# Reordering the head and the layer boundary of a two-layer decoder trunk, with constant products on TensorE in its gaps

## The reference

```python
mod = silu(c) @ w_ada + b_ada                       # 1024 x 3072 per layer
shift, scale, gate = split(mod, 3)
h = rms_norm(x, norm_g) * (1.0 + scale) + shift
proj = h @ w_in                                     # q | k | v | za | u | zs
ya = attend(rope(q), rope(k), v, sinks)             # window 128, with sinks
ys = s5_branch(u, state, a_re, a_im, log_dt, b, c, d, w_glu, b_glu)   # complex diagonal SSM + GLU
x = x + gate * (concat(ya * silu(za), ys * silu(zs)) @ w_out)
```

## Time and profile before

| | us |
|---|---|
| median of 3 runs | 403.86 |
| lowest, highest | 399.94, 405.77 |
| the profiled execution | 400.8 |
| its span, first to last instruction | 399.0 |
| TensorE busy in it | 359.9 |
| VectorE busy | 316.1 |
| ScalarE busy | 197.2 |
| GpSimd busy | 64.8 |

### The profile page before, as it was taken

One profiled execution on the slowest core, in us unless ns is written; L12 is line 12 of the kernel. 1 busy time (PEld: TensorE's weight loads), 2 busy tenths in 40 slices (PEclk: granted clock), 3 DMA queues, 4 the chain that ended last, 5 costly groups with the idle time before them and its releaser, 6 DMA issues. The chain is left out here.

```text
span 399.0 us, 8243 instructions
## 1 busy us (share of the span) xinstructions
PE 359.9 (90%) x3122; PEld 313.2 (79%) x3122; DVE 316.1 (79%) x676; ACT 197.2 (49%) x423; POOL 64.8 (16%) x58
## 2 busy tenths in 40 slices
PE   0997589998999799999999759999999999899993
PEld 0462379987979597977989758999997988779992
DVE  1648889977899958898599876889699589976863
ACT  2365255365463117787335556427633177863432
POOL 3200000020000370000499800000000000002430
PEclk9999969999999899999999959999999999999998
DMA  8999826799839966953995072391998279522303
GB/s 247 292 349 369 203 60 229 244 169 204 264 101 267 268 176 168 352 125 92 294 301 103 2 235 67 91 167 46 287 176 214 45 202 334 142 64 59 100 2 131
DMA packets 125125, 72.27 MB, mean 181 GB/s; under 512 B 63385, under 2 KB 111605, under 8 KB 124990
## 3 DMA queue, kind: packets, MB, share of 16 engines
q1 hardware_dynamic: 111118, 65.05, 61.3%
q10 hardware_dynamic: 13968, 6.69, 7.3%
HBM read 64.74 MB, written 6.59 MB: 179 GB/s over the span
## 5 line engine op out<-in xcount | busy, mean ns | idle before, releaser
L691 PE MATMUL bank<-h_hi,w_hi 128*128 128x320 f32 x448 | 138.6, 322 | 13.0 <-DVE h_lo L1906 10.7
L691 PE MATMUL bank<-h_lo,w_hi 128*128 128x320 f32 x448 | 134.4, 312 | 0.0
L691 PEld LDWEIGHTS bank<-h_hi,w_hi 128*128 128x128 f32 x448 | 85.6, 191 | 21.0 <-issue 12.4
L691 PEld LDWEIGHTS bank<-h_lo,w_hi 128*128 128x128 f32 x448 | 85.7, 191 | 0.2
L691 PE MATMUL bank<-h_hi,w_lo 128*128 128x320 f32 x448 | 81.8, 312 | 0.0
L1702 DVE TENSOR_TENSOR w_lo<-raw,w_hi 128x1024 fp32r<-128x1024 f32 x50 | 63.0, 1259 | 10.7 <-ACT w_hi L1272 10.4
L691 PEld LDWEIGHTS bank<-h_hi,w_lo 128*128 128x128 f32 x448 | 70.9, 191 | 0.0
L1272 ACT ACTIVATE w_hi<-raw 128x1024 fp32r<-128x1024 f32 x50 | 52.7, 1053 | 31.0 <-DMA raw<-in_w_in 16.9
L2304 POOL TENSOR_TENSOR ga<-xT,fing 128x320 f32<-128x320 f32 x4 | 6.5, 1632 | 141.8 <-DVE xT L2185 141.8
L1452 ACT ACTIVATE R<-R,sm 128x128 f32<-128x128 f32 (+2 forms) x40 | 17.7, 443 | 9.6 <-issue 5.7
L691 PE MATMUL bank<-R,Gm 128*128 128x96 f32 x128 | 17.4, 297 | 3.8 <-DVE R L2039 3.8
(11 more groups left out here) (321 smaller groups left out, 638.1 us busy)
## 6 DMA issues: line engine op xcount, KB each, us to landing
R<-in_w_ada SPq DMA_DIRECT2D x34, 512.0 KB, 6.6
raw<-in_w_in SPq DMA_DIRECT2D x32, 256.0 KB, 5.9
raw<-in_w_in SPq DMA_DIRECT2D x14, 512.0 KB, 6.2
raw<-in_w_out SPq DMA_DIRECT2D x32, 128.0 KB, 3.6
raw<-in_w_out SPq DMA_DIRECT2D x16, 256.0 KB, 4.0
raw<-in_w_ada SPq DMA_DIRECT2D x4, 512.0 KB, 8.2
R<-in_w_in SPq DMA_DIRECT2D x4, 512.0 KB, 11.4
raw<-in_w_glu SPq DMA_DIRECT2D x4, 512.0 KB, 4.4
```

The source lines that it names most:

```text
L691: return nc.tensor.matmul(out_, lhsT, rhs, start=start, stop=stop, skip_group_check=free)
```

## The change

- **SyncE's queue:** ss0 and ss1 go behind the ten small loads; ss0 to ss7 stand together; the two loads of B (256 KB each) go from before ss6 to behind ss11.
- **TensorE, constant products:** `stay_busy(bank, n, cols)` multiplies the constant `mean` (128 x 128) by constants into a bank whose next job overwrites it. 12 of 128 columns stand ahead of c's turning, 5 of 128 ahead of x's, 3 of 512 ahead of `carried(0)` in layer 0, and at the boundary 1 of 512 ahead of `sum_squares`, 1 ahead of `spread_root` and 2 behind it.
- **TensorE, order:** `spread_root` after five chunks; `turn_modulation(0, 0)` right behind it; u0 and u1's tiles 0, 1 after ss7, tiles 2, 3 after ss9; B is turned after u0 and u1 are done, in the `work` ring. WB blocks of layer 0 are turned two each behind u3, q0, q1, q2.
- **ScalarE:** both am0 and am1 are copied out before w_hi of u0 and u1; the exponential of `ssm_sines` and the sines stand between am2 and am3; `inputs_B` comes behind u0's copy.
- **VectorE:** one more pair of squares is added ahead of `first_squares`, which has two products per group for three. Angles, `normed` of tiles 4 to 7 and `powers` stand between tiles 3 and 4; only four small operations (`denominators`) stand ahead of `normed`. `higher_powers` goes behind all tiles of h, followed by w_lo of u2, `inputs_scaled`, the four `turned_inputs`, and `wide_powers` last. In layer 1 `normed` is done two tiles at a time.
- **Sums of squares in both layers:** the last square is no longer added by VectorE; TensorE adds it with a third product per group.

```diff
+TURNED_AFTER = ({"u3": (0, 1), "q0": (2, 3), "q1": (4, 5), "q2": (6, 7)},
...
             sp.dma_start(crow[1:CT, :], a["c_sample"]).then_inc(cond_in, 16)
-            for m in range(2):
-                load(0, f"ss{m}")
...
-            for m in range(2, 6):
+            for m in range(8):
+                load(0, f"ss{m}")
+            sp.wait_ge(*work.ready(0, "cT"))
+            load(0, "u0")
+            load(0, "u1")
+            for m in range(8, 12):
                 load(0, f"ss{m}")
             for r, name in enumerate(("ssm_b_re", "ssm_b_im")):
...
-            for m in range(6, 8):
-                load(0, f"ss{m}")
-            sp.wait_ge(*work.ready(0, "cT"))
-            load(0, "u0")
-            load(0, "u1")
-            for m in range(8, 16):
+            for m in range(12, 16):
                 load(0, f"ss{m}")
...
+            def stay_busy(bank, n, cols=512):
+
+                for _ in range(n):
+                    mm(bank[:, 0:cols], mean[:, :], (const if cols > P else mean)[:, 0:cols], True, True)
+
+            pe.wait_ge(mean_set, 1)
+            b = work.bank(0, "cT")
+            stay_busy(b, 12, P)
...
             ins.then_inc(work.filled(0, "cT"), 1)
+            stay_busy(work.bank(0, "xT0"), 5, P)
             pe.wait_ge(x_in, 32)
...
                     mm(o, sqsum[:, toks], mean[:, 0:1], True, False)
+                    mm(o, sq[:, 0, toks], mean[:, 0:1], False, False)
                     ins = mm(o, sq[:, 1, toks], mean[:, 0:1], False, True)
...
                     first_squares()
-                    turn_inputs_B()
-                    for m in range(2, 4):
+                    for m in range(2, 5):
                         modulation(0, f"ss{m}")
                     spread_root(0)
-                    for m in range(4, 8):
+                    turn_modulation(0, 0)
+                    for m in range(5, 8):
                         modulation(0, f"ss{m}")
-                        if m == 5:
-                            turn_modulation(0, 0)
                     turn_modulation(0, 1)
-                    for m in range(8, 12):
-                        modulation(0, f"ss{m}")
                     project_two(0, ("u0", "u1"), range(2), True)
-                    turn_modulation(0, 2)
-                    for m in range(12, 14):
+                    for m in range(8, 10):
                         modulation(0, f"ss{m}")
                     project_two(0, ("u0", "u1"), range(2, 4), True)
-                    for m in range(14, 16):
+                    for m in range(10, 12):
+                        modulation(0, f"ss{m}")
+                    turn_modulation(0, 2)
+                    for m in range(12, 16):
                         modulation(0, f"ss{m}")
                     turn_modulation(0, 3)
                     project_two(0, ("u0", "u1"), range(4, KT), False)
+                    turn_inputs_B()
                     turn_inputs_C()
...
+                    pe.wait_ge(*work.room(l, "rms"))
+                    stay_busy(work.bank(l, "rms"), 1)
                     sum_squares(l, "rms", l + 1)
...
+                    pe.wait_ge(*proj.room(l, "u0"))
+                    stay_busy(proj.bank(l, "u0"), 1)
                     spread_root(l)
+                    stay_busy(proj.bank(l, "u0"), 2)
                     project_two(l, ("u0", "u1"), range(KT), True)
...
+                pe.wait_ge(*work.room(l, "y0"))
+                if l == 0:
+                    stay_busy(work.bank(l, "y0"), 3)
                 pe.wait_ge(H_ready, (l + 1) * 2)
...
             def ssm_sines():
 
                 act.wait_ge(ssm_exp, 3)
+                fn(zz[:, 6, :], zz[:, 4, :], ACT.Exp).then_inc(ssm_val, 1)
...
                 if l == 0:
-                    inputs_B()
                     modulation_rows(0, 0)
-                    ssm_sines()
+                    modulation_rows(0, 1)
                     hi_part(0, 0)
-                    modulation_rows(0, 1)
                     hi_part(0, 1)
                 for pair in range(0, KT, 2):
-                    if l == 0 and pair in (2, 4):
-                        modulation_rows(0, 2 if pair == 2 else 3)
+                    if l == 0 and pair == 4:
+                        modulation_rows(0, 2)
+                        ssm_sines()
+                        modulation_rows(0, 3)
...
                 newton(l + 1)
                 if l == 0:
-                    powers()
+                    denominators()
                 dve.wait_ge(*work.ready(l, "rb"))
...
-                    if pair == 4:
+                    if l:
+                        normed((pair, pair + 1))
+                    elif pair == 4:
+                        angles()
                         normed(range(4, KT))
                         if l == 0:
-                            higher_powers()
+                            powers()
                             modulation_of(0, 2)
                             modulation_of(0, 3)
...
                 if l == 0:
+                    higher_powers()
+                    lo_part(0, 2)
                     inputs_scaled()
+                    for m in range(4):
+                        if m:
+                            lo_part(0, m + 2)
+                        turned_inputs(m)
                     wide_powers()
-                    for m in range(4):
-                        lo_part(0, m + 2)
-                        turned_inputs(m)
...
-                    if m:
+                    if 0 < m < KT - 1:
                         add_square(m - 1, (l + 1) * KT + m)
```

More of the change, by code:

```diff
@@ L134 @@
 ADA_JOBS = AM_JOBS[:4] + [(0, "sinks")] + AM_JOBS[4:]
[L135 removed]
+TURNED_AFTER = ({"u3": (0, 1), "q0": (2, 3), "q1": (4, 5), "q2": (6, 7)},
                 {"out7": (0, 1, 2, 3), "rms": (4, 5), "u1": (6, 7)})
 def proj_jobs():
[L141 removed]
+    return ([(l, job) for l in range(DEPTH) for job in PROJ_LAYER]
             + [(DEPTH, job) for job in LAST_PROJ_JOBS])
@@ L152, in work_jobs @@
             jobs += [(l, "rms"), (l, "rb")]
-            jobs += [(0, f"at{x}") for x in range(4)] + [(0, f"CT{n}") for n in range(4)]
-            jobs += [(l, x) for x in ("WB0", "WB1", "WB2", "WB3", "WB4", "WB5", "rope0", "WB6", "rope1", "WB7", "h0",
+            jobs += [(0, f"at{x}") for x in range(4)] + [(0, "BT0"), (0, "BT1")] + [(0, f"CT{n}") for n in range(4)]
+            jobs += [(l, x) for x in ("WB0", "WB1", "WB2", "WB3", "rope0", "WB4", "WB5", "rope1", "WB6", "WB7", "h0",
                                       "rope2")]
@@ L579, in load_quad @@
                 if (own, x) == (1, 0):
-                    sp.wait_ge(*proj.ready(0, "BT1"))
+                    sp.wait_ge(*work.ready(0, "BT1"))
                     sp.wait_ge(sinks_turned, 1)
@@ L719, in turn_inputs_B @@
                 for n in range(2):
-                    b = proj.bank(0, f"BT{n}")
+                    pe.wait_ge(*work.room(0, f"BT{n}"))
+                    b = work.bank(0, f"BT{n}")
                     for c in range(8):
@@ L723, in turn_inputs_B @@
                         ins = nc.tensor.transpose(b[:, c * 64:(c + 1) * 64], src, ident[0:64, 0:64])
-                    ins.then_inc(proj.filled(0, f"BT{n}"), 1)
+                    ins.then_inc(work.filled(0, f"BT{n}"), 1)
             def turn_inputs_C():
@@ L1228, in inputs_B @@
                 for n in range(2):
-                    act.wait_ge(*proj.ready(0, f"BT{n}"))
-                    src = proj.bank(0, f"BT{n}")[:, :].rearrange("p (c w) -> p w c", c=8)
+                    act.wait_ge(*work.ready(0, f"BT{n}"))
+                    src = work.bank(0, f"BT{n}")[:, :].rearrange("p (c w) -> p w c", c=8)
                     for r in range(2):
@@ L1234, in inputs_B @@
                         if r == 1:
-                            ins.then_inc(proj.emptied(0, f"BT{n}"), 1)
+                            ins.then_inc(work.emptied(0, f"BT{n}"), 1)
                         else:
                             step.add(ins)
+                step.wait()
             def inputs_C():
@@ L1795, in inputs_scaled @@
             def inputs_scaled():
-                dve.wait_ge(*proj.taken(0, "BT1"))
+                dve.wait_ge(*work.taken(0, "BT1"))
                 for r in range(2):
@@ L1883, in _ @@
                     lo_part(0, 1)
-                else:
-                    normed(range(4))
                 for pair in range(0, KT, 2):
-                    if pair == 4:
+                    if l:
+                        normed((pair, pair + 1))
+                    elif pair == 4:
+                        angles()
                         normed(range(4, KT))
                         if l == 0:
-                            higher_powers()
+                            powers()
                             modulation_of(0, 2)
```

54 lines of the change are left out of this document (27 added, 27 removed).

## The result

The changed kernel takes 411.94 us (median; 410.33 to 413.12), the kernel before beside it 402.75 (399.94 to 405.77): a ratio of 1.022, interval 1.014 to 1.031. It is slower by about 9 us. The forecast was 397.7 and its range ended at 403.5.

A forecast was written before the change was run, and what follows sets the result against it. TensorE was taken to bound the end, VectorE the pace up to 135.58 us. Scan's end -4.5, carried -1.7, boundary -0.5 and tail +0.5 gave -6.2 us: 397.7 against the median 403.86, range 391 to 403.5.

The forecast's parts named there:

- A change that moves little can win only in its gaps: Whole kernel: gains only in TensorE's gaps and low-clock stretches; up to 135.58 us VectorE sets the pace.
- x and the clock: Head: x 2.5 us earlier without ss0 and ss1 beside it; constant products lift the clock, root spread near 18 us.
- rival 2: Constant products do not lift the clock, or it falls again among ss0 to ss4: -1.5 us, 402.4; chance 21%.
- The last mod at 41.2: Head: last mod ready at 41.2 us, not 48.95, a gain of 7.75 us.
- the prediction's own decision point: Head: rival 3 decides as soon as the last mod comes after 43.9 us (48.95 - 5.04).
- rival 3: higher_powers behind the last h_lo makes the kernel slower: +3.6 us, 407.5; chance 7%.
- That is -2.5 at q2: Before the scan: q2's low part moves by -7.75 + 5.04 + 0.2 = -2.5 us.
- B is turned only after u0 and u1 ... 0.2 taken: Before q2: inputs_scaled may wait up to 0.8 us for B; 0.2 taken.
- Slack taken up, 2.0: VectorE before the scan: earlier loads remove 2.0 us of its 5.9 idle, bounds 0 and 4.4.
- Carried, -1.7: Gap before layer 0's carried: three constant products hold the clock, saving half of 3.40 us, -1.7.
- Boundary, -0.5: Boundary: faster spreading at the upper clock, -0.5 us at even odds, bounds 0 to -0.9.
- Tail, +0.5: Tail: the sum for rmsF takes half as much again, less 0.15 us of addition; +0.5, uncovered.

The follow-up runs named there:

- sinks_early: The changed kernel with the sinks' bank emptied on VectorE behind the second of the four turned inputs, not behind wide_powers; 411.38 us, ratio 1.022.
- quiet: The changed kernel without any of its constant products; 413.79 us, ratio 1.021.
- after: First profile of the changed kernel, nothing else altered; profiled execution 412.6 us, span 410.8 us.
- after_again: The changed kernel unaltered, run once more for a second profile; 413.74 us, one execution.
- no_head_products: The changed kernel without the head's 17 constant products, the other 7 kept; 416.61 us, one execution.
- sines_first: The changed kernel with the exponential, sines and their table loads on ScalarE ahead of the copy of am2; 408.60 us, ratio 1.009.
- higher_behind: b_early with higher_powers moved back behind the last h_lo, ahead of everything else on VectorE; 406.32 us, ratio 1.008.
- mended: The changed kernel with angles, sines, powers, higher_powers, ss10 and ss11 earlier, sinks early, old boundary, 3 products before carried in both layers; 406.76 us, ratio 1.012.
- b_early: mended with B turned ahead of tiles 4 to 7, copied before u0 and scaled before u2's low part; 399.64 us, ratio 0.988.
- scan_only: The kernel before with only the 3 constant products ahead of carried in layer 0; 402.10 us, ratio 0.997.
- bound_only: The kernel before with only the change's boundary part: normed in pairs, third product, one addition less, 4 constant products; 405.46 us, ratio 1.002.
- first profile of before: First profile of the kernel before, unaltered, the reference of the comparisons; profiled execution 400.8 us, span 399.0 us.
- before_again: The kernel before unaltered, run once more for a second profile; 405.46 us, one execution.
- carried_both: The changed kernel with the 3 constant products ahead of carried in layer 1 too; 410.01 us, ratio 1.014.

## Why the prediction was wrong

**"A change that moves little can win only in its gaps": right.** VectorE does set the pace up to the scan. sinks_early shows it once more: taking away a TensorE wait of 3.76 us brought no gain that shows.

**x and the clock: right in the main.** x starts 1.4 us earlier and not 2.5, and that is the order of the loads, since it does so without the products too (8.85 in quiet). The constant products lift the clock: twelve transpositions of x take 2.35 us in after and 3.72 in quiet. The first low parts come 6.5 to 7.6 us earlier with them, 1.3 to 1.6 without (u1: after, after_again against quiet, no_head_products). But the clock does not stay. It is at 0.66 over 18.00 to 23.00, where the root is spread, and ss7, which had landed at 19.2 (8.99 + 10.2), is multiplied only at 23.78; the forecast had 20 to 21. It is at 0.50 at 28.83, through the first tiles, and h_lo of tiles 0 to 3 ends at 33.5 (32.63 + 0.89 in VectorE's timeline) and not at 30.4. It fell again in the sparse stretch, as rival 2 had it for another price.

**The last mod at 41.2: the step that failed.** I worked it out as two chains, the sines behind VectorE's angles and am3 behind ss15's landing, and never priced am2. It is in neither: TensorE reaches ss10 and ss11 only behind tiles 2 and 3, ScalarE waits for them 6.27 us, and the sines stand behind that copy, though the angles were ready at 36.48. The exponential's table load starts at 39.84 where I had 33.3: 3.2 us of that are the late first tiles, 3.4 the wait for am2. Powers follow at 43.05 and not at 36.5, and the last mod at 46.84. The other chain failed in the same way: ss15's landing was forecast at 38.5 and came at 37.0, but its products run only from 41.4 on, behind ss10 to ss13. So even with the sines out of the way am3 would have come late, and in sines_first VectorE does wait for it. What the sum lacked is TensorE's own turn at the chunks.

**"That is -2.5 at q2": right as a sum, wrong by its input.** The last h_lo moved from 53.68 to 51.34: -2.34, plus 5.04 for higher_powers, is +2.7; q2's low part was +2.67. So the prediction's own decision point (a last mod beyond 43.9) decided, for rival 3, to which I gave 7%. higher_behind shows its price in isolation.

**"B is turned only after u0 and u1 ... 0.2 taken": right in this order.** The wait is 0.00 in after and 0.91 in after_again, against 0.2 with a bound of 0.8. It is small because higher_powers stands in front of it. mended, which takes higher_powers away, has 5.93 us of it and of u2's high part; with B ahead as well (b_early) the gain gets through. So the order that the change gives up had two merits, higher_powers in a wait and B early, and giving back one alone brings little: at q2, mended and higher_behind, with one each, are 1.3 and 1.5 us ahead of after, and b_early, with both, is 4.1 ahead.

**Slack taken up, 2.0: 0.6** (q2 to zs1, +2.67 to +2.04), because nothing came sooner. In b_early it is 1.6.

**Carried, -1.7: right** (-1.3 after, -1.7 scan_only, clock 1.00). **Boundary, -0.5: the term is right where it stands alone** (-0.7 in bound_only), but in after it is +2.3 from zs3 to u2, 1.5 of which is the fall of the clock at 192.67; after_again +2.2 without that fall. The clock there did improve (0.50 for 3.41 us and not 10.20), and nothing of that reached u2. Why the boundary itself varies so, I leave open. **Tail, +0.5: 0.7** (11.8 less 11.1).

**Layer 1 was missing altogether: +8.1 us,** +3.4 through za3 and +4.7 behind it, in the stretch that holds carried and both falls of the clock, at 312.14 and 332.60. Nothing in the code of that part had changed, so I gave it no term and no rival. That is why even rival 3, whose mechanism came true, ended at 407.5 and not at 412. It is the larger part of the loss, and what makes za3's load late is open. With +2.0 at the scan, -1.3, +2.3, +8.1 and +0.7 the account closes at the 11.8 us between the spans; some 2 us of these are the good luck of the first profile of before.

**The clock's worth.** Of the falls that the changed kernel has and the first profile of before has not, the one at 192.67 stands beside a loss of 1.5 us (out2), and the two in layer 1 beside 4.7 us. By an estimate, 6.8 us at the lower level are 3.4 us of doubled time, and the rest of the 4.7 would be the fall at 332.60. That is 6.2 us, or 1.5% of the span; the 3 products of layer 0 saved 1.7. How much of it belongs to the kernel, two profiles do not settle: after_again has the 6.8 us behind carried but not the falls at 192.67 and 332.60, and before_again has falls of its own. By the Trainium skill ("TensorE: Matmul & The Clock Gate", "What's actually happening") the ramp's penalty is under 1% of a span and varies from run to run. That the clock's cost varies, the profiles show; the falls inside this kernel cost more than that by the estimate. The table load came at 1.28 us twice, as in the earlier trace rows, the exponential and the sine right behind it. "ScalarE: Activation LUTs" ("What ACT_TABLE_LOAD costs") in the Trainium skill gives 2.66 us for a switch, the load and a drain; the drain does not show here (39.84 + 1.28, and the exponential at 41.13).

## What to carry to other kernels

When a function is moved out of a wait, list what the wait was covering and what the function will cover in its new place, and price every producer of what was waited for, not only the two that look longest. Here the sum had no line for TensorE's own turn at the chunks, and an experiment that moved higher_powers back without B laid bare 5.93 us of other waits. A wait on an engine that is ahead can be worth nothing: 3.76 us on TensorE came back as 4.41 us one unit later. Read who is late behind it. And take two profiles of each kernel before explaining differences under 2 us between them.

## What was not expected of the hardware

A change that touches the first 10 us of TensorE's work went together with a DMA 280 us later that took 6.8 to 10.5 us in all twelve profiles with it and 4.6 to 5.3 in six of seven without. And where TensorE idled 2.67 us in front of layer 1's carried (2.71 in after_again) and not 0.92, the clock then stood at the lower level for 6.8 us and not at all; constant products in that gap held it at 1.00 in carried_both and mended.
